# Modulation and h by pairs of feature chunks, context sums later, convolution taps spilled into the attention loop

## The reference

```
m_lat = silu(c) @ w_mod + b_mod          # shift, scale, gate for the latent tokens
m_ctx = silu(c_ctx) @ w_mod + b_mod      # the same for the context
h  = rmsnorm(x) * (1 + sc1) + sh1        # 512 x 1024
hc = rmsnorm(ctx) * (1 + sc1c) + sh1c    # 256 x 1024
proj = h @ w_in                          # q, k, v, glu, gate a, gate b
kv_c = hc @ w_in[:, K0:GLU0]
att = neighbourhood attention of 8 heads over a window of latent keys and all 256 context keys
conv: u = a * sigmoid(g); 31 taps depthwise over positions; layernorm; silu; @ w_conv_out
x_mid = x + g1 * ((sigmoid(ga) * (att @ w_att_out) + sigmoid(gb) * conv) @ w_o)
```

## Time and profile before

| | us |
|---|---|
| median of 3 runs | 1723.99 |
| lowest and highest | 1723.98, 1724.35 |
| profiled execution | 1721.53 |
| its span | 1719.8 |
| TensorE busy | 1590.6 (92%) |
| VectorE busy | 1205.8 (70%) |
| ScalarE busy | 867.3 (50%) |

### The profile page before, as it was taken

One profiled execution on the slowest core, in us unless ns is written; L12 is line 12 of the kernel. 1 busy time (PEld: TensorE's weight loads), 2 busy tenths in 40 slices (PEclk: granted clock), 3 DMA queues, 4 the chain that ended last, 5 costly groups with the idle time before them and its releaser, 6 DMA issues. The chain is left out here.

```text
span 1719.8 us, 21145 instructions
## 1 busy us (share of the span) xinstructions
PE 1590.6 (92%) x7674; PEld 1305.0 (76%) x7674; DVE 1205.8 (70%) x1599; ACT 867.3 (50%) x1104; POOL 218.8 (13%) x169
## 2 busy tenths in 40 slices
PE   7999899979959999999999999397999799999995
PEld 5789678867858888888888887375866588888883
DVE  7787966636359999999999998375666834334346
ACT  2422243462258888888888887332333523222222
POOL 0000000000021534333343432000000000000000
PEclk8999999989969999999999999598999899999998
DMA  8242344423358999999999996632111132323201
GB/s 321 86 159 82 109 147 155 169 73 108 137 206 312 362 375 363 383 372 377 370 370 368 365 376 233 224 108 95 50 49 50 59 102 87 100 94 98 98 25 49
DMA packets 121585, 329.46 MB, mean 192 GB/s; under 512 B 12730, under 2 KB 80442, under 8 KB 96818
## 3 DMA queue, kind: packets, MB, share of 16 engines
q1 hardware_dynamic: 110450, 311.59, 49.7%
q0 software_dynamic: 11072, 17.03, 2.9%
HBM read 332.48 MB, written 20.99 MB: 206 GB/s over the span
## 5 line engine op out<-in xcount | busy, mean ns | idle before, releaser
L1589 PE MATMUL moe_bank<-moe_expert_lo,moe_x_hi 128*128 128x512 f32 x512 | 202.9, 396 | 3.6 <-DVE moe_x_lo L1497 3.6
L1590 PE MATMUL moe_bank<-moe_expert_hi,moe_x_lo 128*128 128x512 f32 x512 | 200.1, 391 | 0.0
L1591 PE MATMUL moe_bank<-moe_expert_hi,moe_x_hi 128*128 128x512 f32 x512 | 199.9, 391 | 0.0
L1938 ACT ACTIVATE second_c_hi<-second_c_raw 128x2048 fp32r<-128x2048 f32 x44 | 84.0, 1909 | 161.8 <-PE second_bank L2393 160.4
L2391 PE MATMUL second_bank<-second_cx_lo,second_c_hi 128*128 128x512 f32 x352 | 140.8, 400 | 15.4 <-DVE second_cx_lo L2088 10.0
L1491 DVE TENSOR_TENSOR moe_expert_lo<-kq,moe_expert_hi 128x2048 fp32r<-128x2048 f32 x62 | 141.8, 2287 | 16.2 <-ACT moe_expert_hi L1289 16.1
L1491 DVE TENSOR_TENSOR moe_expert_lo<-vals,moe_expert_hi 128x2048 fp32r<-128x2048 f32 x62 | 141.7, 2288 | 9.3 <-ACT moe_expert_hi L1289 9.3
L832 PE MATMUL mixer_bank<-mixer_h_lo,mixer_w_hi 128*128 128x512 f32 x320 | 131.8, 412 | 11.5 <-DVE mixer_h_lo L582 11.5
L2392 PE MATMUL second_bank<-second_cx_hi,second_c_lo 128*128 128x512 f32 x352 | 138.1, 392 | 0.0
L2393 PE MATMUL second_bank<-second_cx_hi,second_c_hi 128*128 128x512 f32 x352 | 138.1, 392 | 0.0
L2391 PE MATMUL second_bank<-g_lo,second_c_hi 128*128 128x512 f32 x320 | 127.4, 398 | 1.2 <-DVE g_lo L2226 1.2
(11 more groups left out here) (411 smaller groups left out, 3484.2 us busy)
## 6 DMA issues: line engine op xcount, KB each, us to landing
vals<-in_w_exp_up_dram SPq DMA_DIRECT2D x62, 1024.0 KB, 7.8
kq<-in_w_exp_down_dram SPq DMA_DIRECT2D x62, 1024.0 KB, 7.3
second_c_raw<-in_w_mlp_dram SPq DMA_DIRECT2D x32, 1024.0 KB, 5.1
work<-in_w_exp_gate_dram SPq DMA_DIRECT2D x31, 1024.0 KB, 7.1
moe_shared<-in_w_exp_gate_dram SPq DMA_DIRECT2D x31, 1024.0 KB, 7.2
mixer_raw<-in_w_in_dram SPq DMA_DIRECT2D x18, 1024.0 KB, 5.0
mixer_raw<-in_w_mod_t_dram SPq DMA_DIRECT2D x16, 1024.0 KB, 4.9
second_c_raw<-in_w_in_dram SPq DMA_DIRECT2D x8, 1024.0 KB, 8.6
```

The lines of the kernel that those rows point to most:

```text
L1589: pe.matmul(out, x_hi[s][:, c, :], lo[:, k, :], start=(h == 0 and k == 0), stop=False)
L1590: pe.matmul(out, x_lo[s][:, c, :], hi[:, k, :], start=False, stop=False)
L1591: ins = pe.matmul(out, x_hi[s][:, c, :], hi[:, k, :], start=False, stop=(h == 1 and k == 3))
```

## The change

- The unit of c for VectorE (`c_wide`, `cctx_wide`) is no longer spread by TensorE but loaded 128 times over from the host, and taken through Silu on ScalarE; the context half comes last. Units 0, 1, 2 (the shift of chunks 0 to 5) go to TensorE, 4, 5, 6, 3, 7 to VectorE (scale, and the last pair's shift and scale), and at first for c alone. The dot products for c_ctx follow behind tiles 0 to 3.
- The sum of squares of x gives a column a token block (64 records of one column); its inverse root is taken on 128x4, spread as a diagonal and multiplied with ones (one 512-column product), and x is multiplied in place (`x_normed`).
- h goes by pairs of chunks: `pair_columns(p)`, `h_pair(p)` on ScalarE (now scale and shift at once, then the high part), `h_low`. `first_tiles` takes the first four tiles chunk by chunk as pairs arrive, with `modulation(2)` between.
- SP loads splits 0 and 1 early, between the units. The context's squares are summed after split 2.
- Of the taps 89 stand before the loop and 7 each in iterations 0 to 4 (TAPS_IT). The sum of taps moves from iteration 0 to 5, of squares from 2 to 8, the normalisation to 11 to 14. The late units leave iterations 0 to 4; the table LATE puts two into 5, 8, 10 and 15 and one into the others. The turns of the attention output go from iterations 6, 10, 14 to 9, 13, 15.
- Buffers are laid out anew (`early`, `turned`, `u_pad`, `sig`, `att`).

The diff, cut to its core:

```diff
+        TAPS_IT = 5
+        LATE = {5: 2, 6: 1, 7: 1, 8: 2, 9: 1, 10: 2, 11: 1, 12: 1, 13: 1, 14: 1, 15: 2, 16: 1}
+
+        def late_units(n):
+            first = 8 + sum(LATE[i] for i in LATE if i < n)
+            return range(first, first + LATE.get(n, 0))
+
         RING = [("split", s) for s in range(12)]
         for n in range(N_IT + 2):
             RING += [("split", s) for s in (splits_after(n - 1) if n else [])]
-            if n < N_IT:
-                RING.append(("mod", 8 + n))
+            RING += [("mod", u) for u in late_units(n)]
...
+        BY_PE = (0, 1, 2)
+        BY_DVE = (4, 5, 6, 3, 7)
+        TURN_ATT = {9: 0, 13: 1, 15: 2}
...
-            sp.dma_start(c_row, w["c_row"]).then_inc(c_landed, 16)
             sp.dma_start(cols[:], w["cols"]).then_inc(cols_landed, 16)
+            sp.dma_start(c_wide[:], w["c_wide"][:, 0:D]).then_inc(c_landed[0], 16)
...
+            def early_split(u):
+                sp.dma_start(as_k8(raw[u][:]), w_in[:, :, SPLITS[u][1]:SPLITS[u][1] + 256]).then_inc(raw_landed[u], 16)
...
             early_unit(0)
-            early_unit(1)
-            early_unit(2)
             for half in range(2):
                 sp.dma_start(x_mid[:, 4 * half:4 * half + 4, :], x_tc[:, 4 * half:4 * half + 4, :])\
                   .then_inc(xt_landed[half], 16)
-            for u in range(3, 8):
-                early_unit(u)
+            early_unit(4)
+            early_split(0)
+            early_unit(1)
+            early_unit(5)
+            early_split(1)
+            early_unit(2)
+            early_unit(6)
+            sp.wait_ge(xssq_ready, 1)
+            early_unit(3)
+            early_unit(7)
+            sp.dma_start(cctx_wide, w["c_wide"][:, D:2 * D]).then_inc(c_landed[1], 16)
+            sp.dma_start(ctx_t, c_t).then_inc(ct_landed, 16)
...
+            def h_pair(p):
+                act.wait_ge(s1_ready, p + 1)
+                for c in (2 * p, 2 * p + 1):
+                    act.wait_ge(xn_done, c + 1)
+                    if c >= 2:
+                        act.wait_ge(hlo_done, c - 1)
+                    act.activation(tmp[c % 2], x_mid[:, c, :], ACT.Identity, scale=s1[:, c:c + 1],
+                                   bias=mod_col[:, c:c + 1]).then_inc(tmp_ready, 1)
+                for c in (2 * p, 2 * p + 1):
+                    act.wait_ge(tmp_ready, c + 1)
+                    act.activation(h_hi[:, c, :], tmp[c % 2], ACT.Copy).then_inc(hhi_done, 1)
...
+            for p in range(1, 4):
+                h_pair(p)
+            act.wait_ge(c_landed[1], 16)
+            act.activation(cctx_wide, cctx_wide, ACT.Silu).then_inc(silu_ready, 1)
...
+            def pair_columns(p):
+
+                dve.wait_ge(early_done, sums[0])
+                if p in BY_PE:
+                    dve.wait_ge(pe_mod_done, BY_PE.index(p) + 1)
+                    dve.tensor_tensor(mod_col[:, 2 * p:2 * p + 2], pe_sum[p][:, :, 0],
+                                      cols[:, V_BMOD + 2 * p:V_BMOD + 2 * p + 2], ALU.add)
+                    at = 8 + 2 * p
+                    step(dve.tensor_tensor(mod_col[:, at:at + 2], early_sum[:, at:at + 2, 0],
+                                           cols[:, V_BMOD + at:V_BMOD + at + 2], ALU.add))
...
+            def x_normed(c):
+                dve.tensor_tensor(x_mid[:, c, :], x_mid[:, c, :], bank[4][:], ALU.mult).then_inc(xn_done, 1)
...
+            unit_sum(4, 0, 0)
+            dve.wait_ge(xssq_ready, 1)
+            dve.tensor_scalar(rs_col[:], bank[5][:, 0:TC], 1.0 / D, NORM_EPS, ALU.mult, ALU.add).then_inc(xvar_ready, 1)
+            unit_sum(4, 1, 0)
...
+            pair_columns(0)
...
+            low(0)
+            h_low(0)
+            h_low(1)
+            x_normed(2)
+            x_normed(3)
+            for f in range(2):
+                unit_sum(5, f, 0)
+            pair_columns(1)
             low(1)
+            h_low(2)
+            h_low(3)
+            x_normed(4)
+            x_normed(5)
+            for f in range(2):
+                unit_sum(6, f, 0)
+            pair_columns(2)
+            x_normed(6)
+            x_normed(7)
+            h_low(4)
+            h_low(5)
+            for u in (3, 7):
+                for f in range(2):
+                    unit_sum(u, f, 0)
+            pair_columns(3)
+            dve.wait_ge(silu_ready, 3)
+            h_low(6)
+            h_low(7)
...
-            TAPS_AFTER = {1: 11, 2: 22, 3: 32, 4: 50, 5: 68, 6: 86, 7: 104, 8: 115, 9: len(taps)}
+            TAPS_AFTER = {3: 6, 4: 24, 5: 43, 6: 62, 7: 73, 8: 84, 9: 89}
+            TAPS_IN = [89 + 7 * n for n in range(TAPS_IT + 1)]
...
+                    for u, f in ctx_sums[:2]:
+                        unit_sum(u, f, 1)
                 if READER[names[s]] == "dve":
                     glu_tiles(s)
                 low(s + 2)
+                if s == 1:
+                    for u, f in ctx_sums[2:]:
+                        unit_sum(u, f, 1)
+                    ctx_columns()
...
-                    late_unit(8 + n)
+                for u in late_units(n):
+                    late_unit(u)
                 if 1 <= n <= N_IT:
                     turned_odd(n - 1)
-                if n >= 7 and n % 4 == 3:
-                    att_low(n // 4 - 1)
-                if n == 1:
+                if n < TAPS_IT:
+                    convolve(TAPS_IN[n], TAPS_IN[n + 1])
...
+                for t in range(TC):
+                    ins = pe.matmul(bank[5][:, t:t + 1], sq_lat[:, c, 128 * t:128 * t + 128], ones[:, 0:1],
+                                    start=(c == 0 and t == 0), stop=(c == KC - 1 and t == TC - 1))
             ins.then_inc(xssq_ready, 1)
-            modulation(BY_PE[1])
-            modulation(BY_PE[2])
+            pe.wait_ge(diag_ready, 1)
+            pe.matmul(bank[4][:], ones[:], diag, start=True, stop=True).then_inc(rs_ready, 1)
+            modulation(1)
...
+            first_tiles((0, 1), (0, 1))
+            first_tiles((0, 1), (2, 3))
+            modulation(2)
+            first_tiles((2, 3), (0, 1))
+            first_tiles((2, 3), (2, 3))
+            first_tiles((4, 5), (0, 1))
+            first_tiles((4,), (2, 3))
+            first_tiles((6, 7), (0, 1))
+            first_tiles((5, 6, 7), (2, 3))
+            for s in range(2, 10):
...
-                if n >= 6 and n % 4 == 2:
-                    turn_att(n // 4 - 1)
-                if n == 0:
+                if n in TURN_ATT:
+                    turn_att(TURN_ATT[n])
+                if n == TAPS_IT:
```

More of the change, by code:

```diff
@@ L90, in mixer_stage @@
         V_BMOD, V_NORM, V_CB, V_CG, V_CO = 0, 48, 56, 60, 64
[L92 to L93 removed]
+        early = [vals[:, 2048:4096], flex[:, 2048:4096], flex[:, 0:2048], kq[:, 0:2048],
+                 table[:, 1024:3072], table[:, 3072:5120], flex[:, 4096:6144], kq[:, 2048:4096]]
         gc_hi = g_hi[:, 0:4, :].rearrange("p a (b t) -> p (a b) t", t=CTX)
@@ L373, in _ @@
                            cols[:, 244:260].rearrange("p (s k) -> p s k", s=2), ACT.Silu).then_inc(silu_ready, 1)
-            act.wait_ge(wide_ready, 1)
-            for b in range(4):
-                dst = (c_wide if b < 2 else cctx_wide)[:, 512 * (b % 2):512 * (b % 2) + 512]
-                act.activation(dst, bank[b][:], ACT.Silu).then_inc(silu_ready, 1)
+            act.wait_ge(c_landed[0], 16)
+            act.activation(c_wide[:], c_wide[:], ACT.Silu).then_inc(silu_ready, 1)
             for c in range(KC):
@@ L589, in h_low @@
-                ins.then_inc(hlo_done, 1)
-            def h_chunks(first):
-                for c in range(first, first + KC):
-                    if c >= 2:
-                        dve.wait_ge(hlo_done, c - 1)
-                    h_scaled(c)
-                    if c > first:
-                        h_low(c - 1)
-                    elif first == 0:
-                        low(0)
-                h_low(first + KC - 1)
-            h_chunks(0)
-            low(1)
-            dve.wait_ge(xssq_ready, 2)
@@ new lines, in _ @@
+            unit_sum(4, 1, 0)
+            dve.wait_ge(xstd_ready, 1)
+            step(dve.reciprocal(rs_col[:], rs_col[:]))
+            dve.wait_ge(ident_ready, 2)
+            dve.tensor_tensor(diag.rearrange("p (t q) -> p t q", t=TC), ident[:].unsqueeze(1).to_broadcast([P, TC, P]),
+                              rs_col[:].unsqueeze(2).to_broadcast([P, TC, P]), ALU.mult).then_inc(diag_ready, 1)
+            pair_columns(0)
+            dve.wait_ge(rs_ready, 1)
+            for half in range(2):
+                dve.wait_ge(xt_landed[half], 16)
@@ L607, in glu_tiles @@
+            ctx_sums = [(u, f) for u in BY_DVE for f in range(2)]
             def glu_tiles(s):
@@ L644, in _ @@
                 low(s + 2)
+                if s == 1:
+                    for u, f in ctx_sums[2:]:
+                        unit_sum(u, f, 1)
+                    ctx_columns()
+                if s == 2:
+                    dve.wait_ge(xssq_ready, 2)
```

(15 more changed lines are left out.)

241 lines of the change are left out of this document (120 added, 121 removed).

## The result

| | before | changed |
|---|---|---|
| median (runs) | 1723.99 (4, 1717.75 to 1724.35) | 1738.94 (4, 1736.72 to 1739.92) |
| ratio to before | 1 | 1.0117, interval 1.0097 to 1.0137 |
| span of the profiled execution | 1719.8 | 1738.1 |
| end of the attention loop in it | 360.6 | 376.9 |
| from there to the end | 1359.2 | 1361.2 |

The changed kernel is slower, by some 15 us in the medians and 18.3 in the profiled executions, where 6.3 were forecast. Of the 18.3 us, 16.3 stand at the end of the attention loop. The other 2.0 are in code that the change doesn't touch; over the twelve profiles of this study that part takes 1354.5 to 1362.6 us, so they say nothing.

The account below looks back on a forecast made before the run. TensorE, busy 92% of the span, was taken as the bound; -0.6 - 3.6 + 2.0 + 7.0 + 1.5 = +6.3 us moved the median from 1723.99 to 1730.3, range 1725 to 1735.5.

Parts of the forecast that it names:

- A: Opening, through the first four tiles and the context squares: ends at 73.6 against 74.2, -0.6 us.
- E: Iterations 15 and 16 of the attention loop: late units and a low part waiting for its transfer, +1.5 us.
- term of 1.6 us for a fall: Cost of TensorE's clock falling during a long wait: 1.6 us in the opening and iteration 10, half in iteration 5.
- D: Iteration 10: two late units behind a low part make TensorE wait 5.9 us, with a clock fall; +7.0 us.
- C: Iteration 5: two late units behind a low part, wait 3.0, today's gaps -1.8, clock +0.8; +2.0 us.
- B: Taps around the loop's start: 7.5 us at the tap sum saved, new waits of 2.6 and 1.3; -3.6 us.
- the clock falls in more places: Rival: clock also falls through iteration 5 in full, or modulation unit 2 runs at half pace; +3.5, 1733.8 us, chance 0.20.
- disputed price of the table: Opening, ScalarE's table load before the context Silu: 1.28 us taken; rival adds a drain, +1.4, 1731.7 us, chance 0.03.

Follow-up runs that it names:

- a0_after: The changed kernel run again with no edit, as the reference of the follow-up group: 1.0120 of the kernel before.
- e2_late: Changed kernel with only the table LATE altered, so no pair of late units shares an iteration with a split's low part (15 excepted): 1.0028 of the kernel before.
- e8_place: Changed kernel with its own table LATE; in iterations with a low part the late units stand behind VectorE's copy of the turned tile: 1.0014 of the kernel before.
- the best kernel here: Changed kernel with silu wait moved, LATE without pairs beside low parts, squares added on VectorE, late unit behind the copy, taps moved: 0.9899 of the kernel before.

## Why the forecast was right in place and wrong in size

Every wait that was forecast is in the trace at its place: 3.76 for 4 to 5 in the opening, 2.50 for 2.6, 1.24 for 1.3, 3.21 for 3.0, 5.90 for 5.9, and the tap sum without its 5.78. The direction was right. The total missed by 10 us, in three terms: the clock, the opening (A) and the loop's end (E).

**The clock, 5.7 of the 10.** The failing step is the term of 1.6 us for a fall. It was read from the gap of 3.75 ahead of L832, where eight products are slow; inside the loop the three falls lasted two to three times as long and cost 3.2 to 3.8. And it was put at only one place in full (D), half at C and nowhere in B, where the two new waits of 2.50 and 1.24 brought one of 3.3. That a wait in the loop brings a fall stood in the profile of before: the wait of 5.78 was followed by a sum of 5.27 instead of 3.60. Its price there, 1.8, was no better a guide to the size. The rival "the clock falls in more places" named the mechanism, with 3.5 us for all of it.

**A, 3.1.** Forecast -0.6, measured +2.5 at the first scores (189.18 against 186.67); 2.1 of it stands at split 2 already (73.28 and 3.3 us of context squares at 84.31, against 74.4). Three sizes were off. The 64 one-column records took 13.8 us, where 12.4 were taken, and started 0.5 later, so that VectorE could multiply x by the inverse root 2.5 later (33.57 for 31.1). VectorE's waits from there to the last pair were 3.2 (2.26 and 0.91) where 1.4 stood for all: modulation 2 on TensorE, for which it waited 2.26, queued behind records and products at half pace. And the silu wait was 4.99 where 4.6 were taken. The luck of no fall gave 1.6 back, and a0_after shows that it is as a rule not given. The reading behind the first size was wrong too: the row of 64 records in 8.61 is a mixture, 49 at 0.11 until the clock falls at 31.1 and 15 at 0.21 behind it, so at the half level 64 cost 13.7, and no row stood for 12.4. What the rows also show, and no run tests: the kernel before reaches the full pace at 20.9, in its 16 wide squares, while the changed one has only narrow records (and two wide ones) until 40.0 and reaches it at 43.7. On the disputed price of the table, the row has the load at 62.76 for 1.28 and the next activation at 64.06: no drain, as the forecast took it. The Trainium skill speaks for both: "ScalarE: Activation LUTs", section "What ACT_TABLE_LOAD costs", would have the wait 1.4 longer (an estimate from its drain of 1380 ns), while "ScalarE activation tables: per-element evaluation and per-set limits", section "What a function is on this engine", has 1283 ns between functions of different sets; this case's traces agree with the second.

**B.** -3.6 forecast, -3.7 by the rows up to values(0) (24.0 us before; 16.9 after, and the moved sum of 3.4 comes later). Its clock is counted above.

**C and D without the clock.** The waits were right within 0.2, and e2_late and e8_place confirm their cause. The argument stopped one step early, though: it named the buffer as the cause, while e8_place shows that the same late transfer is harmless where the copy stands ahead of it.

**E, 1.1.** Forecast +1.5, measured +2.6 from values(9) to the loop's end, clock left out. The waits there are 0.89, 0.88, 0.54 and 0.78 (330.88 to 368.89) against 0.89 and 0.45 before, so +1.75. The other 0.85 is in part one turn of the attention output more in that stretch; the rest isn't assigned.

The three make 9.9 of the 10; the rest is rounding of these readings.

## What to carry to other kernels

Price a new wait of a saturated TensorE as itself plus a stretch at half clock, and take that second part from a wait inside the same kind of work, not from one at a stage's end: here it was about as large as the waits themselves (6.4 beside 6.6). Behind a step that waits for a transfer, look what else is queued on its engine: moving one copy ahead of the late units took the changed kernel from 1.0117 to 1.0014, as much as the best kernel here gains on the kernel before. And before a chain of tiny matmuls becomes the head of a stage, look whether an idle engine can add first, so that TensorE has an eighth of them to do.

## What the runs showed of the hardware

One- and two-column records have two prices, and these are the two levels of the clock. In the changed kernel the first 32 two-column records, 64 one-column ones (13.8 us) and the next 32 (6.83, at 33.32) all run at 0.21 each. The 32 at 47.31 take 3.93: 0.11 each until 50.4, then 0.21. The granted clock falls there:

```profile
50.00:52.00 2.00, 2.00 (x11) 0.62 0.00 0
52.00:54.00 2.00, 2.00 (x6) 0.53 0.00 0
```

The 64 of the kernel before turn from 0.11 to 0.21 at 31.1, where its clock falls: the window of 30 to 32 us reads 0.78, the next one 0.50.

Ahead of 43.66 us the column shows 1.00 all the same, also at 40 to 43.6 us, where fp32r products start 0.43 apart instead of 0.23:

```profile
43.15 0.63 PE L925 MATMUL mixer_bank<-mixer_h_hi,mixer_w_lo 128*128 128x512 f32 x1
43.57 0.43 PE L926 MATMUL mixer_bank<-mixer_h_hi,mixer_w_hi 128*128 128x512 f32 x1
...
44.07 0.40 PE L925 MATMUL mixer_bank<-mixer_h_hi,mixer_w_lo 128*128 128x512 f32 x1
44.31 0.40 PE L926 MATMUL mixer_bank<-mixer_h_hi,mixer_w_hi 128*128 128x512 f32 x1
```

That 1.00 is no reading. The trace holds no clock record before 43.66 (before 20.90 in the kernel before), and a window without one prints 1.00. In all twelve profiles TensorE's pace doubles at the first record. So in the opening TensorE works at the pace of the half level, and there the distance of two products tells it, not the column.

And the kernel before spread over 12 us (0.7%) between executions on one chip, as much as a single edit here is worth (0.1 to 1.0%); four runs of it had shown 0.4.
